# Attention by pairs of heads: head pairs in both halves of the matmul array, spread over query and gate panels

## The chip, the cores and the metric

One core of a Trainium2 chip runs the whole program. Its engines are TensorE (PE, matmuls into the eight PSUM banks; PEld in the profile is its weight load), VectorE (DVE), ScalarE (ACT), GpSimd (POOL) and SyncE (SP, which issues the large DMAs). Each engine works through its own list of instructions in order and waits on semaphores. The metric is the device time of one execution in microseconds; lower is better.

## The reference

Three blocks in fp32 on 256 tokens with 2048 features: a state-space layer, a sliding-window attention with shared keys and values, and a second model with neighbourhood attention and a large MLP. The change touches the sliding-window attention alone: 32 heads of 64 features, four key heads, window 128, so that the first 128 queries see 128 keys and the second 128 queries see 256.

```python
def _swa_sink_attention(q, k, v, sinks):
    ...
    s = jnp.einsum("bcqhrd,bckhd->bchrqk", qb, kk).astype(jnp.float32) * (hd ** -0.5)
    ...
    s = jnp.where(valid[None, :, None, None], s, -jnp.inf)
    sk = sinks.astype(jnp.float32)[None, None, :, :, None, None]
    m = jnp.maximum(jnp.max(s, axis=-1, keepdims=True), sk)
    p = jnp.exp(s - m)
    p = p / (jnp.sum(p, axis=-1, keepdims=True) + jnp.exp(sk - m))
    o = jnp.einsum("bchrqk,bckhd->bcqhrd", p.astype(vv.dtype), vv)
    return o.reshape(bsz, seqlen, hk * rq * hd)

def _swa_mixer(x, k, v, cos, sin, w_in, q_bias, sinks, w_out):
    bsz, seqlen, _ = x.shape
    proj = x @ w_in
    q = (proj[..., :Q_WIDTH] + q_bias).reshape(bsz, seqlen, KV_HEADS, Q_PER_KV, ATT_HEAD_DIM)
    gate = proj[..., Q_WIDTH:]
    q = _rope_partial(q, cos[:, :, None, None, :], sin[:, :, None, None, :])
    o = _swa_sink_attention(q, k, v, sinks.reshape(KV_HEADS, Q_PER_KV))
    o = o * jax.nn.silu(gate)
    return o @ w_out
```

## The kernel before

All large products go by weight **units**: 256 rows by 512 columns of weights, 512 KB. A unit lands in `raw` (a ring of four, `RING`), ScalarE rounds it into `whi` (`split_hi`), VectorE takes the rest into `wlo` (`split_lo`), and TensorE multiplies: high by high, high by low and low by high, so that fp32 precision comes from three passes of the faster format. A panel of 512 columns is eight units (`UPP`). A **token unit** (`token_unit`) has tokens in the rows of the output, 12 matmuls of 512 columns; a **feature unit** (`feature_unit`) has features in the rows, 24 matmuls of 256. The two accumulators, banks 0 and 1 and banks 2 and 3, take turns by panel. ScalarE rounds unit u + 4 when TensorE is done with unit u, which frees the place; VectorE follows.

The stage of the change is, in order: four query panels (32 token units), four gate panels (32 feature units), and the first panel of the output projection (`wo`, 8 token units), whose left operand is the gated attention output in `xh` and `xl`.

Before, the queries of all 32 heads are gathered in `qt`; VectorE adds the bias to each panel and rotates all of them at the end (`rotate`). Then attention runs in **slots**, one for each unit of gate and output panel: slot j is unit j of these 40, and after its matmuls TensorE does a piece of attention. Slot 2 turns all keys and queries to feature rows (`qk_turn`, 40 transposes, copied by ScalarE in `qk_by_feature`). Head h starts in slot h + 3: `scores(h)` puts the mask into a bank (4 or 5) by a product with the identity and adds the scores by products over 64 rows of the array, the upper or lower half by the parity of h. VectorE takes the row maxima (`maximum`), ScalarE the exponentials from the bank with their sums (`weights`), VectorE divides (`scaled_weights`). Two slots later TensorE turns the weights into bank 6 (`weights_turned`, three transposes), VectorE copies them (`weights_by_key`), and a slot later the value products fill half of the rows of bank 7 (`values`), a head to 64 columns of the array. ScalarE keeps a pair's output (`output_kept`), VectorE multiplies it with the activated gate (`gated`), and the pair of `gated_hi` and `gated_lo` splits it for the output projection, from slot 31 on.

The order is written out by hand, as numbers of slots in `HEAD0`, `GATED_AT` and `SPLIT_AT`; the loops over j at the end of each engine's stage walk them. An fp32 product of the scores or values is one instruction in the program's order and two passes on TensorE; a transpose is one.

Of the kernel before, what the change touches and what calls it, by code (L numbers as in the profile page):

```python
# [28 lines left out]
F32R = mybir.dt.float32r  # L29
# [5 lines left out]
P = 128  # L35
# [126 lines left out]
def program(nc, xT, x, pos, conv_w, conv_b, dt_bias, a_log, d_skip, norm_w, w_in, w_out, kv_w, kv_b, b_in,  # L162
# [3 lines left out]
    with es:  # L166
# [23 lines left out]
        identr = place("identr", [P, P], F32R)  # L190
# [11 lines left out]
        mask = place("mask", [P, 3 * P], F32R)  # L202
# [36 lines left out]
        maskf = place("maskf", [P, 3 * P], at=yh_at + 4 * KT * T)  # L239
# [29 lines left out]
        oT = place("oT", [P, KT, T], at=R)  # L269
# [3 lines left out]
        qT = place("qT", [P, AH // 2, T])  # L273
        kT = place("kT", [P, KVH, T])
        Pm = place("Pm", [P, 2, 3 * P])
# [3 lines left out]
        rope = [place(f"rope{n}", [P, TT, AH, HALF]) for n in range(4)]  # L279
# [3 lines left out]
        mx = place("mx", [P, AH, 2])  # L283
        nm = place("nm", [P, AH, 2])
        rs = place("rs", [P, AH, 2])
        esk = place("esk", [P, AH, 2])
        rden = place("rden", [P, AH, 2])
# [205 lines left out]
        def _(pool):  # L493
            g = Steps(S("pool_step"))
            a = g.done(pool.memset(ident[:], 0.0))
            b = g.done(pool.memset(maskf[:], 0.0))
# [17 lines left out]
            for n, op, sign in ((0, ALU.is_ge, -1), (1, ALU.is_gt, 1), (2, ALU.is_ge, -1)):  # L514
                v = maskf[:, n * P:(n + 1) * P]
                pool.affine_select(out=v, in_=v, compare_op=op, fill=NEG, base=0, pattern=[[sign, P]],
                                   channel_multiplier=-sign)
# [90 lines left out]
            norm_rows(1, GATE + 2, 4, "ln1_in")  # L608
# [57 lines left out]
        def _(act):  # L666
# [22 lines left out]
            act.wait_ge(S("ident_ready"), 1)  # L689
            act.activation(identr[:], ident[:], ACT.Copy)  # L690
            act.activation(mask[:], maskf[:], ACT.Copy).then_inc(S("constr_ready"), 1)
# [142 lines left out]
            splits(Q, 4)  # L834

# [8 lines left out]
            def qk_by_feature():  # L844
                for n in range(2 + AH // 4):
                    act.wait_ge(S("qk_mm"), n + 1)
                    dst = tile(kT, 2 * n, 2) if n < 2 else tile(qT, 2 * (n - 2), 2)
                    act.activation(dst, ps[:, 4 + n % 4, :], ACT.Copy).then_inc(S("qk_turned"), 1)

            def weights(h):  # L850


                act.wait_ge(S("nm_ready"), h + 1)
                wait(act, "pt_ready", h - 1)
                b = 4 + h % 2
                act.activation(Pm[:, h % 2, 0:P], ps[:, b, 0:P], ACT.Exp, bias=nm[:, h, 0:1], scale=SWA_SCALE,
                               accum_out=rs[:, h, 0:1])
                act.activation(Pm[:, h % 2, P:3 * P], ps[:, b, P:3 * P], ACT.Exp, bias=nm[:, h, 1:2], scale=SWA_SCALE,
                               accum_out=rs[:, h, 1:2])

                act.activation(esk[:, h, :], nm[:, h, :], ACT.Exp, bias=snk[:, h:h + 1]).then_inc(S("p_ready"), 1)

            def output_kept(n):

                act.wait_ge(S("o_done"), 2 * n + 2)
                act.activation(oT[:, n, :], ps[:, 7, (n % 2) * T:(n % 2 + 1) * T], ACT.Copy).then_inc(S("o_read"), 1)
# [5 lines left out]

            for j in range(ASLOTS):
                h = j - HEAD0
                split_hi(act, GATE + RING + j, 0)
                if j == HEAD0 - 1:
                    qk_by_feature()
                if j == GATE_UNITS - 1:

                    act.wait_ge(S("unit_done"), WO)  # L880
                    gated_hi(0)
                    gated_hi(1)
                if 0 <= h < AH:
                    weights(h)
                if 4 <= h and h % 2 == 0 and h // 2 - 2 < AH // 2:
                    output_kept(h // 2 - 2)
                if j % UPP == 0 and 0 < j <= GATE_UNITS:
                    gate_silu(j // UPP - 1)
                if j >= GATE_UNITS:
                    for n, at in enumerate(SPLIT_AT):  # L890
                        if at == j:
                            gated_hi(n)
# [157 lines left out]
        def _(pe):  # L1050
# [218 lines left out]
            token_panels(Q, L_Q, 4, 0)  # L1269
            def qk_turn():  # L1270

                pe.wait_ge(S("rope_done"), 1)
                for n in range(2 + AH // 4):

                    wait(pe, "qk_turned", n - 3)
                    for e in range(2):
                        for m in range(TT):
                            src = kd[:, m, 2 * n + e].rearrange("p a b -> p (a b)") if n < 2 else \
                                qt[:, m, (2 * (n - 2) + e) * P:(2 * (n - 2) + e + 1) * P]
                            last = pe.transpose(ps[:, 4 + n % 4, e * T + m * P:e * T + (m + 1) * P], src, ident[:])  # L1280
                    last.then_inc(S("qk_mm"), 1)
# [852 lines left out]
```

## Time and profile before

| | |
|---|---|
| median of 3 runs | 2247.25 us (2246.58 to 2249.1) |
| the profiled execution | 2246.58 us, its span 2244.8 us |
| TensorE busy | 2194.2 us, 98% |
| VectorE busy | 1342.5 us, 60% |
| ScalarE busy | 1070.9 us, 48% |
| mean granted TensorE clock | 0.995 |

The span runs from the first to the last instruction. The profile gives busy time of each engine and, in the timeline, the start and the duration of each instruction. Matmuls are pipelined: a duration of 0.39 us may stand beside starts 0.23 us apart, so costs on TensorE are read from start to start. A name such as `ps` is the PSUM tensor with all eight banks.

### The profile page before, as it was taken

The page shows a single profiled execution, that of the slowest core. Times are in us where ns is not written, and L with a number is a line of the kernel's source. Part 1 is how long each engine was busy: PE and PEld are TensorE (multiplying, and loading weights), DVE is VectorE, ACT ScalarE, POOL GpSimd, SP SyncE. Part 2 cuts the span into 40 slices and gives each one's busy share as a digit, 9 for nine tenths or more (in the row PEclk, how much of TensorE's full clock was granted, in tenths as well). Part 3 has the DMA queues.
Part 4 walks back from the last instruction along what each step waited for, and adds up shares of the span by engine and source line. Part 5 has one row for each costly group of instructions (what it writes and reads, how often), then busy time and mean ns, then how long its engine had stood idle before and what let it go on. Part 6 is the DMA issues. An engine that isn't in the chain of part 4 may idle for free.

```text
span 2244.8 us, 36327 instructions
## 1 busy us (share of the span) xinstructions
PE 2194.2 (98%) x13614; PEld 1953.9 (87%) x13614; DVE 1342.5 (60%) x1731; ACT 1070.9 (48%) x1407; POOL 130.7 (6%) x136
## 2 busy tenths in 40 slices
PE   7999999999998999999899999999999999999999
PEld 7999989998887888887788878789989989988987
DVE  5677676776545666665676666655555455554554
ACT  4434357776333435454345455545434444443442
POOL 1000001111000100000005210000000000000000
PEclk9999999999999999999999999999999999999999
DMA  7755655554655764334576644455556556656654
GB/s 229 237 177 177 188 188 179 179 171 160 228 192 173 229 195 132 112 112 152 168 216 195 191 139 138 133 189 171 183 196 186 179 195 187 182 192 189 184 188 159
DMA packets 207026, 402.45 MB, mean 179 GB/s; under 512 B 16132, under 2 KB 18308, under 8 KB 206676
## 3 DMA queue, kind: packets, MB, share of 16 engines
q1 hardware_dynamic: 199168, 385.92, 55.2%
q0 software_dynamic: 4096, 14.50, 2.0%
q8 instruction: 64, 1.05, 0.2%
q10 hardware_dynamic: 3668, 0.73, 0.2%
q14 instruction: 30, 0.25, 0.0%
HBM read 395.27 MB, written 5.83 MB: 179 GB/s over the span
## 4 chain that ended last, share of the span: by engine, by line
PE 90%; DVE 4%; ACT 3%; issue 1%; DMA 1%; POOL 1%; ACTq 0%; SPq 0%; DVEq 0%
PE ps L383 16%; PE ps L385 15%; PE ps L384 15%; PE ps L368 12%; PE ps L370 12%; PE ps L369 12%; ACT whi L350 1%; DMA raw<-w_in 1%; PE ps L1128 1%; DVE wlo L355 1%; PE ps L1315 1%; PE ps L1220 1%; PE ps L1295 1%; PE ps L1294 1%; PE ps L1391 1%
## 5 line engine op out<-in xcount | busy, mean ns | idle before, releaser
L355 DVE TENSOR_TENSOR wlo<-raw,whi 128x1024 fp32r<-128x1024 f32 x712 | 875.4, 1234 | 753.0 <-ACT whi L350 748.6
L350 ACT ACTIVATE whi<-raw 128x1024 fp32r<-128x1024 f32 x712 | 753.0, 1059 | 1071.2 <-PE ps L385 593.6
L368 PE MATMUL ps<-xh,whi 128*128 128x256 f32 x2560 | 734.7, 287 | 17.5 <-DVE wlo L355 16.2
L369 PE MATMUL ps<-xl,whi 128*128 128x256 f32 x2560 | 726.2, 284 | 0.0
L370 PE MATMUL ps<-xh,wlo 128*128 128x256 f32 x2560 | 726.0, 284 | 0.0
L368 PEld LDWEIGHTS ps<-xh,whi 128*128 128x128 f32 x2560 | 492.6, 192 | 28.0 <-issue 20.7
L369 PEld LDWEIGHTS ps<-xl,whi 128*128 128x128 f32 x2560 | 492.9, 193 | 0.2
L370 PEld LDWEIGHTS ps<-xh,wlo 128*128 128x128 f32 x2560 | 492.8, 192 | 0.0
L383 PE MATMUL ps<-whi,xh 128*128 128x512 f32 x792 | 318.7, 402 | 5.8 <-DVE xl L1871 3.1
L384 PE MATMUL ps<-wlo,xh 128*128 128x512 f32 x792 | 310.0, 391 | 0.0
L385 PE MATMUL ps<-whi,xl 128*128 128x512 f32 x792 | 309.9, 391 | 0.0
L383 PE MATMUL ps<-whi,ah 128*128 128x512 f32 x512 | 199.3, 389 | 0.0
L384 PE MATMUL ps<-wlo,ah 128*128 128x512 f32 x512 | 199.3, 389 | 0.0
L385 PE MATMUL ps<-whi,al 128*128 128x512 f32 x512 | 199.3, 389 | 0.0
L383 PEld LDWEIGHTS ps<-whi,xh 128*128 128x128 f32 x792 | 149.6, 189 | 38.5 <-DVE xl L1871 3.7
L385 PEld LDWEIGHTS ps<-whi,xl 128*128 128x128 f32 x792 | 149.6, 189 | 32.3
L384 PEld LDWEIGHTS ps<-wlo,xh 128*128 128x128 f32 x792 | 149.8, 189 | 30.2
L385 PEld LDWEIGHTS ps<-whi,al 128*128 128x128 f32 x512 | 96.2, 188 | 20.0
L384 PEld LDWEIGHTS ps<-wlo,ah 128*128 128x128 f32 x512 | 96.2, 188 | 19.8
L383 PEld LDWEIGHTS ps<-whi,ah 128*128 128x128 f32 x512 | 96.2, 188 | 19.8
L383 PE MATMUL ps<-whi,yh 128*128 128x512 f32 x248 | 96.8, 390 | 0.0
L384 PE MATMUL ps<-wlo,yh 128*128 128x512 f32 x248 | 96.5, 389 | 0.0
(243 smaller groups left out, 1651.1 us busy)
## 6 DMA issues: line engine op xcount, KB each, us to landing
raw<-w SPq DMA_DIRECT2D x256, 512.0 KB, 3.6
raw<-w_in SPq DMA_DIRECT2D x160, 512.0 KB, 4.2
raw<-w_qkv SPq DMA_DIRECT2D x96, 512.0 KB, 4.3
raw<-w_out SPq DMA_DIRECT2D x64, 512.0 KB, 3.7
raw<-b_in SPq DMA_DIRECT2D x64, 512.0 KB, 4.3
raw<-b_out SPq DMA_DIRECT2D x32, 512.0 KB, 3.8
raw<-w_o SPq DMA_DIRECT2D x32, 512.0 KB, 3.6
cumb<-cum_scratch SPq DMA_DIRECT2D x16, 512.0 KB, 4.2
```

Source lines behind the costliest of these rows:

```text
L350: act.activation(whi[:, u % RING], raw[:, u % RING], ACT.Copy).then_inc(S("hi_ready"), 1)
L355: dve.tensor_tensor(wlo[:, u % RING], raw[:, u % RING], whi[:, u % RING].bitcast(F32), ALU.subtract).then_inc(S("lo_ready"), 1)
L368: pe.matmul(o, w_h, ah[:, k, :], start=(k == 0 and n % 2 == 0), stop=False, skip_group_check=True)
L369: pe.matmul(o, w_h, al[:, k, :], start=False, stop=False, skip_group_check=True)
L370: last = pe.matmul(o, w_l, ah[:, k, :], start=False, stop=(k == KT - 1), skip_group_check=True)
L383: pe.matmul(o, x_h, whi[:, u % RING, t, :], start=(k == 0), stop=False)
L384: pe.matmul(o, x_h, wlo[:, u % RING, t, :], start=False, stop=False)
L385: last = pe.matmul(o, x_l, whi[:, u % RING, t, :], start=False, stop=(k == kts - 1))
L1128: last = pe.matmul(ps[r:r + HD, 3, c0 + lo:c0 + hi], xc[:, g % 2, k, f:f + HD], m, start=first, stop=not first, skip_group_check=True)
L1220: last = pe.transpose(ps[:, 4 + kp % 4, n * T + m * P:n * T + (m + 1) * P], src[:, m, k * P:(k + 1) * P], ident[:])
L1294: pe.matmul(ps[:, b, 0:P], q_[:, 0:P], k_[:, 0:P], start=False, stop=True, skip_group_check=True)
L1295: pe.matmul(ps[:, b, P:3 * P], q_[:, P:T], k_, start=False, stop=True, skip_group_check=True).then_inc(S("s_ready"), 1)
```

## The change

Heads go by pairs, and attention begins in the query panels. There are now 72 slots, over query, gate and first output panel. Each query panel is given its bias and rotated as soon as it is done (`query_panel`). Keys are turned in slot 9. Pair p has its scores in slot 12 + 3p, its queries turned three slots before (into bank 6, copied by ScalarE to one of two places of `qT`), its weights turned four and five slots after, its values six slots after. The scores of both heads stand in turn in the list, from the two row halves into banks 4 and 5; those of the values from the two column halves into bank 7. The mask is no longer a product on TensorE: VectorE adds it while it moves the scores of both heads from the banks to `Pm`, where ScalarE takes the exponentials in place. The copy of turned weights (`weights_by_key`) moves from VectorE to ScalarE. The normalising pieces of the rows (`norm_row`) move from query panels 2 and 3 to the slots 32 to 47. The gated outputs 0 to 5 are split in slots 57 to 62 and the last two in slot 66; before, two of them in slot 31, two in 32, two in 33 and one each in 35 and 38, which are output units 0, 1, 3 and 6.

```diff
@@ -77,12 +77,19 @@
-HEAD0 = 3
-ASLOTS = GATE_UNITS + UPP
-
-GATED_AT = [4 * n + HEAD0 + 7 for n in range(AH // 4)]
-SPLIT_AT = [GATE_UNITS - 1, GATE_UNITS - 1, GATE_UNITS, GATE_UNITS, GATE_UNITS + 1, GATE_UNITS + 1, GATE_UNITS + 3,
-            GATE_UNITS + 6]
+AP = AH // 2
+PPK = AP // KVH
+ASLOTS = 2 * GATE_UNITS + UPP
+GATE_AT, WO_AT = GATE_UNITS, 2 * GATE_UNITS
+KEYS_AT, PAIR0, STRIDE = UPP + 1, 12, 3
+SCORES_AT = [PAIR0 + STRIDE * p for p in range(AP)]
...
+TURNED_AT = [(at + 4, at + 5) for at in SCORES_AT]
+VALUES_SLOT = [at + 6 for at in SCORES_AT]
...
@@ -841,29 +837,35 @@
+            def weights(p):
+
+                act.wait_ge(S("nm_ready"), p + 1)
+                for e in range(2):
+                    for c, v in enumerate((Pm[:, p % 2, e, 0:P], Pm[:, p % 2, e, P:3 * P])):
+                        act.activation(v, v, ACT.Exp, bias=nm[:, p, c, e:e + 1], scale=SWA_SCALE,
+                                       accum_out=rs[:, p, c, e:e + 1])
+                act.activation(esk[:, p], skd[:, p], ACT.Exp).then_inc(S("p_ready"), 1)
+
+            def weights_by_key(p, e):
+
+                act.wait_ge(S("pt_ready"), 2 * p + e + 1)
+                wait(act, "o_done", p)
+                act.activation(PTm[:, e], ps[:, 6, 0:3 * P], ACT.Copy).then_inc(S("pts_ready"), 1)
...
-                pe.matmul(ps[:, b, 0:3 * P], identr[:], mask[:], start=True, stop=False,
-                          skip_group_check=True)
-                pe.matmul(ps[:, b, 0:P], q_[:, 0:P], k_[:, 0:P], start=False, stop=True, skip_group_check=True)
-                pe.matmul(ps[:, b, P:3 * P], q_[:, P:T], k_, start=False, stop=True,
-                          skip_group_check=True).then_inc(S("s_ready"), 1)
...
+            def scores(p):
+
+                pe.wait_ge(S("k_turned"), 2)
+                pe.wait_ge(S("q_turned"), p + 1)
+                wait(pe, "s_read", p)
+                for c in range(TT):
+                    for e in range(2):
+                        r = HD * e
+                        q_, k_ = qT[r:r + HD, p % 2, c * P:(c + 1) * P], kT[r:r + HD, p // PPK, 0:(c + 1) * P]
+                        last = pe.matmul(ps[:, 4 + e, c * P:c * P + (c + 1) * P], q_, k_, start=(c == 0), stop=True,
+                                         skip_group_check=True)
+                last.then_inc(S("s_ready"), 1)
...
+            def values(p):
+
+                pe.wait_ge(S("pts_ready"), 2 * p + 2)
+                wait(pe, "o_read", p)
+                k0 = (KVH + p // PPK) * HD
+                c0 = p % 2 * T
+                for m, lo in ((0, 0), (1, P)):
+                    for e in range(2):
+                        r_ = HD * e
+                        w = PTm[:, e, 0:T] if m == 0 else PTm[:, e, T:3 * P]
+                        last = pe.matmul(ps[r_:r_ + HD, 7, c0 + lo:c0 + T], kvt[:, m, k0:k0 + HD], w, start=(m == 0),
+                                         stop=(m == 1), skip_group_check=True)
+                last.then_inc(S("o_done"), 1)
...
+            def maximum(p):
+
+                dve.wait_ge(S("s_ready"), p + 1)
+                wait(dve, "pt_ready", 2 * (p - 1))
+                v = Pm[:, p % 2]
+                s = d.done(dve.tensor_tensor(v, ps[:, 4:6, 0:3 * P], mask[:].unsqueeze(1).to_broadcast([P, 2, 3 * P]),
+                                             ALU.add))
...
             for j in range(ASLOTS):
...
+                split_lo(dve, Q + RING + j, 0)
+                if j < GATE_AT and j % UPP == UPP - 1:
+                    query_panel(j // UPP)
+                for p in range(AP):
+                    if j == SCORES_AT[p]:
+                        maximum(p)
+                    if j == SCORES_AT[p] + 2:
+                        scaled_weights(p)
+                if X1_AT <= j < X1_AT + 2 * UPP:
+                    norm_row(j - X1_AT, "ln0_in", "x1_rows")
```

The lines of the program after the change are numbered one higher for the helpers (L356 for L355 and so on). In the rows below a matmul row stands for one line's product, whose two passes are not told apart.

TensorE, one slot of before in the middle of the gate panels, from the last matmul of the unit on: one head turned, the next but one scored, the one before given its values.

```order
L370 MATMUL ps<-xh,wlo 128x256
L1303 MATMUL ps<-ident,Pm 128x128 [waits pts_ready,p_scaled]
L1303 MATMUL ps<-ident,Pm 128x128 x2
L1292 MATMUL ps<-mask,identr 128x384 [waits p_ready]
L1294 MATMUL ps<-kT,qT 128x128
L1295 MATMUL ps<-kT,qT 128x256
L1315 MATMUL ps<-PTm,kvt 64x256 [waits pts_ready]
L1317 MATMUL ps<-PTm,kvt 64x128
```

TensorE after the change, slot 18, the first with all three: values of pair 0, scores of pair 2, queries of pair 3, then the next unit.

```order
L386 MATMUL ps<-whi,xl 128x512
L1323 MATMUL ps<-PTm,kvt 64x256 [waits pts_ready]
L1323 MATMUL ps<-PTm,kvt 64x256
L1323 MATMUL ps<-PTm,kvt 64x128 x2
L1300 MATMUL ps<-kT,qT 128x128 [waits s_read,q_turned,k_turned]
L1300 MATMUL ps<-kT,qT 128x128
L1300 MATMUL ps<-kT,qT 128x256 x2
L1288 MATMUL ps<-ident,qt 128x128 [waits pts_ready,rope_done]
L1288 MATMUL ps<-ident,qt 128x128
L384 MATMUL ps<-whi,xh 128x512 [waits lo_ready,x_ready]
```

The mask product is gone, the products of two heads stand side by side, and the turn of the weights has gone to the two slots between.

ScalarE before, two slots in the gate panels (names: `Pm` weights, `rs` their sums, `esk` the sink's term, `oT` the output kept).

```order
L856 ACTIVATE Pm,rs<-ps,nm 128x128 [waits nm_ready]
L858 ACTIVATE Pm,rs<-ps,nm 128x256
L861 ACTIVATE esk<-nm,snk 128x2
L866 ACTIVATE oT<-ps 128x256 [waits o_done]
L350 ACTIVATE whi<-raw 128x1024 [waits unit_done,landed2]
L856 ACTIVATE Pm,rs<-ps,nm 128x128 [waits pt_ready,nm_ready]
```

ScalarE after, slots 16 to 18: the exponentials of pair 1 stand between the two copies of turned weights of pair 0.

```order
L351 ACTIVATE whi<-raw 128x1024 [waits unit_done,landed0]
L863 ACTIVATE PTm<-ps 128x384 [waits pt_ready]
L855 ACTIVATE Pm,rs<-Pm,nm 128x128 [waits nm_ready]
L855 ACTIVATE Pm,rs<-Pm,nm 128x256
L855 ACTIVATE Pm,rs<-Pm,nm 128x128
L855 ACTIVATE Pm,rs<-Pm,nm 128x256
L857 ACTIVATE esk<-skd 128x4
L351 ACTIVATE whi<-raw 128x1024 [waits unit_done,landed1]
L863 ACTIVATE PTm<-ps 128x384 [waits pt_ready]
L351 ACTIVATE whi<-raw 128x1024 [waits unit_done,landed2]
L868 ACTIVATE oT<-ps 128x256 [waits o_done]
L848 ACTIVATE qT<-ps 128x256 [waits q_mm]
```

The copies were VectorE's before, and each head's exponentials had a slot of their own; now one slot in three has four of them.

VectorE before, one slot of the gate panels.

```order
L1835 TENSOR_REDUCE mx<-ps 128x1 [waits s_ready]
L1836 TENSOR_REDUCE mx<-ps 128x1
L1838 SCALAR_TENSOR_TENSOR nm<-mx,nsnk 128x2 [waits dve_step]
L1846 COPY PTm<-ps 128x384 [waits o_done,pt_ready]
L355 TENSOR_TENSOR wlo<-raw,whi 128x1024 [waits hi_ready]
```

VectorE after, slot 15: the second query panel stands before the maxima of pair 1.

```order
L1836 TENSOR_TENSOR qt<-ps,qbias 128x512 [waits qb_in1,unit_done]
L1836 TENSOR_TENSOR qt<-ps,qbias 128x512
...
L1799 TENSOR_TENSOR qt<-rope_131,rope_132 128x2x8x8 [waits dve_step]
L1800 TENSOR_TENSOR qt<-rope_133,rope_134 128x2x8x8
L1848 TENSOR_TENSOR Pm<-ps,mask 128x768 [waits dve_step,s_ready]
L1852 TENSOR_REDUCE mx<-Pm 128x2 [waits dve_step]
L1853 TENSOR_REDUCE mx<-Pm 128x2
L1856 SCALAR_TENSOR_TENSOR nm<-mx,nsnk 128x4 [waits dve_step]
L1858 TENSOR_TENSOR skd<-nm,nsnk 128x4 [waits dve_step]
```

The copy is gone and the add with the mask has come; a panel's bias and rotation now lie between a pair's scores and its maxima.

## Rows read from the trace of the kernel before

**Rows 1.** Busy time (and instructions) of each engine, gate panels with attention.

```profile
core 0: us, PE busy (x) PEld busy (x) DVE busy (x) ACT busy (x) POOL busy (x), PEclk, DMA share, GB/s
860.00:1003.00 143.00, 142.98 (x989) 119.86 (x987) 91.42 (x254) 75.48 (x195) 3.75 (x7) 1.00 0.39 117
```

**Rows 2.** Timeline, TensorE: start us, duration, instruction [idle before]; ends of stages, waits.

```profile
752.74 0.39 PE L383 MATMUL ps<-whi,xh 128*128 128x512 f32 x1
...
839.78 0.28 PE L368 MATMUL ps<-xh,whi 128*128 128x256 f32 x1
...
854.66 0.39 PE L368 MATMUL ps<-xh,whi 128*128 128x256 f32 x1 [1.30 <-ACT qT L848]
...
1036.76 0.80 PE L383 MATMUL ps<-whi,xh 128*128 128x512 f32 x1 [3.07 <-DVE xl L1871]
...
1041.14 0.39 PE L383 MATMUL ps<-whi,xh 128*128 128x512 f32 x1
```

**Rows 3.** Timeline, TensorE: one head's slot in the gate panels.

```profile
906.65 0.28 PE L370 MATMUL ps<-xh,wlo 128*128 128x256 f32 x1
906.77 0.49 PE L1303 MATMUL ps<-ident,Pm 128*128 128x128 f32 x3
907.01 0.42 PE L1292 MATMUL ps<-mask,identr 128*128 128x384 f32 x1
907.37 0.48 PE L1294 MATMUL ps<-kT,qT 64*128 64x128 f32 x2
...
908.22 0.65 PE L1315 MATMUL ps<-PTm,kvt 128*64 128x256 f32 x2
...
909.01 0.39 PE L368 MATMUL ps<-xh,whi 128*128 128x256 f32 x1
...
911.98 0.49 PE L1303 MATMUL ps<-ident,Pm 128*128 128x128 f32 x3
```

**Rows 4.** Timeline, TensorE: a pair of heads in the state-space stage.

```profile
504.60 0.28 PE L370 MATMUL ps<-xh,wlo 128*128 128x256 f32 x1
504.80 0.87 PE L1128 MATMUL ps<-Mm,xc 128*64 128x256 f32 x8
505.61 0.39 PE L368 MATMUL ps<-xh,whi 128*128 128x256 f32 x1
```

**Rows 5.** Timeline, TensorE: four transposes in each token slot, key and value panel.

```profile
731.72 0.60 PE L1220 MATMUL ps<-ident,xtok 128*128 128x128 f32 x4
...
734.93 0.60 PE L1220 MATMUL ps<-ident,xtok 128*128 128x128 f32 x4
```

**Rows 6.** Timeline, ScalarE: split, exponentials of a head, output kept.

```profile
907.03 1.06 ACT L350 ACTIVATE whi<-raw 128x1024 fp32r<-128x1024 f32 x1 [1.98 <-PE ps L370]
909.18 0.37 ACT L856 ACTIVATE Pm<-ps,nm 128x128 f32<-128x128 f32 x1 [1.09 <-DVE nm L1838]
...
910.17 0.38 ACT L866 ACTIVATE oT<-ps 128x256 f32<-128x256 f32 x1
```

**Rows 7.** Timeline, VectorE: maxima, copy, split, scaling, gating in one slot.

```profile
908.32 0.29 DVE L1835 TENSOR_REDUCE mx<-ps 128x1 f32<-128x128 f32 x1 [1.94 <-PE ps L1295]
...
909.06 0.56 DVE L1846 COPY PTm<-ps 128x384 f32<-128x384 f32 x1
909.53 1.22 DVE L355 TENSOR_TENSOR wlo<-raw,whi 128x1024 fp32r<-128x1024 f32 x1
910.66 0.15 DVE L1851 TENSOR_TENSOR rs<-rs,esk 128x2 f32<-128x2 f32 x1
...
911.52 0.68 DVE L1865 TENSOR_TENSOR oT<-oT,gT 128x512 f32<-128x512 f32 x1
```

**Rows 8.** Timeline, VectorE: bias and rotation of the key and value panel.

```profile
755.23 1.28 DVE L1770 TENSOR_TENSOR kvt<-ps,kvbias 128x512 f32<-128x512 f32 x2
...
757.72 0.43 DVE L1794 COPY kd<-kvt 128x512 f32<-128x512 f32 x1
```

**Rows 9.** Groups of instructions: busy us, mean ns, idle before; ScalarE's exponential tables.

```profile
L856 ACT ACT_TABLE_LOAD x5 | 6.4, 1283 | 0.1
```

More of the change, by code:

```diff
@@ L201, in program @@
         xl = place("xl", [P, KT, T], F32R)
-        mask = place("mask", [P, 3 * P], F32R)
+        mask = place("mask", [P, 3 * P])
         mask01 = place("mask01", [P, 3 * P])
@@ L278, in program @@
         kvbias = place("kvbias", [P, PANEL])
-        rope = [place(f"rope{n}", [P, TT, AH, HALF]) for n in range(4)]
+        rope = [place(f"rope{n}", [P, TT, PANEL // HD, HALF]) for n in range(4)]
         lnrow = place("lnrow", [P, 2, D])
@@ L1268, in _, with keys_turned @@
             entry_panel(KV, L_KV, 0, 0)
[L1269 to L1275, printed above, removed]
+            def keys_turned():
+                pe.wait_ge(S("k_ready"), 1)
+                for n in range(2):
                     for e in range(2):
                         for m in range(TT):
[L1278 to L1281, printed above, removed]
-                pe.wait_ge(S("qk_turned"), 2 + AH // 4)
@@ L1298, in weights_turned, with queries_turned @@
-            def weights_turned(h):
-                pe.wait_ge(S("p_scaled"), h + 1)
-                wait(pe, "pts_ready", h)
+                            last = pe.transpose(ps[:, 4 + n, e * T + m * P:e * T + (m + 1) * P],
+                                                kd[:, m, 2 * n + e].rearrange("p a b -> p (a b)"), ident[:])
+                    last.then_inc(S("k_mm"), 1)
+            def queries_turned(p):
+                pe.wait_ge(S("rope_done"), p // PPK + 1)
+                wait(pe, "pts_ready", 2 * sum(b < QUERIES_AT[p] for _, b in TURNED_AT))
+                for m in range(TT):
+                    last = pe.transpose(ps[:, 6, m * P:(m + 1) * P], qt[:, m, p * P:(p + 1) * P], ident[:])
+                last.then_inc(S("q_mm"), 1)
@@ new lines, in _ @@
+                if j == KEYS_AT:
+                    keys_turned()
+                for p in range(AP):
+                    if j == VALUES_SLOT[p]:
+                        values(p)
+                    for e in range(2):
+                        if j == TURNED_AT[p][e]:
+                            weights_turned(p, e)
+                for p in range(AP):
+                    if j == SCORES_AT[p]:
+                        scores(p)
+                    if j == QUERIES_AT[p]:
+                        queries_turned(p)
@@ L1793, in _ @@
                     .to_broadcast([P, KVH, 2, HD])
-                dve.tensor_copy(kd[:, m], src)
+                last = dve.tensor_copy(kd[:, m], src)
+            last.then_inc(S("k_ready"), 1)
+            dve.wait_ge(S("mask_ready"), 3)
+            s = d.done(dve.tensor_scalar(nsnk[:], snk[:], -1.0, None, ALU.mult))
+            d.wait(dve, s)
             def norm_row(i, sem, out):
@@ L1854, in scaled_weights @@
                 d.wait(dve, s)
-                for m, v in enumerate((Pm[:, h % 2, 0:P], Pm[:, h % 2, P:3 * P])):
-                    last = dve.tensor_scalar(v, v, rden[:, h, m:m + 1], None, ALU.mult)
+                sink = nsnk[:, 2 * p:2 * p + 2].unsqueeze(1).to_broadcast([P, TT, 2])
+                s = d.done(dve.scalar_tensor_tensor(nm[:, p], mx[:, p], -SWA_SCALE, sink, ALU.mult, ALU.min))
+                d.wait(dve, s)
+                dve.tensor_tensor(skd[:, p], nm[:, p], sink, ALU.subtract).then_inc(S("nm_ready"), 1)
@@ new lines, in scaled_weights @@
+            def scaled_weights(p):
+                dve.wait_ge(S("p_ready"), p + 1)
+                s = d.done(dve.tensor_tensor(rs[:, p], rs[:, p], esk[:, p], ALU.add))
+                d.wait(dve, s)
+                s = d.done(dve.reciprocal(rden[:, p], rs[:, p]))
+                d.wait(dve, s)
+                for c, v in enumerate((Pm[:, p % 2, :, 0:P], Pm[:, p % 2, :, P:3 * P])):
+                    r = rden[:, p, c, :].unsqueeze(2).to_broadcast([P, 2, (c + 1) * P])
+                    last = dve.tensor_tensor(v, v, r, ALU.mult)
```

194 lines of the change are left out of this document (67 added, 127 removed).

## The prediction

> **What bounds the kernel now.** I read the page first: TensorE is busy for 98% of the span, so time can only be won where it does work that isn't needed, does it singly, or stands. The stretch view [rows 1] says the same of the attention stage: TensorE 142.98 of 143.00 us busy at a granted clock of 1.00, VectorE 91 and ScalarE 75. So in this stage neither of the two helpers is the limit; TensorE's own list of instructions is. I then took starts of single matmuls from the timeline, since a start-to-start distance is what an instruction really costs (durations overlap).
>
> The stage from the first query unit to the second output panel runs from 752.74 to 1041.14, 288.40 us [rows 2]. It holds 72 weight units. A token unit costs 2.72 us: 32 of them fill 752.74 to 839.78 [rows 2]. A feature unit is 24 matmuls at a step of 0.12 us [rows 3], 2.88 us. So the units alone need 32 x 2.72 + 32 x 2.88 + 8 x 2.72 = 200.96 us, and **attention costs 87.4 us of TensorE's time on top**. Where those sit:
> - Each head's slot: from the last matmul of the unit, 906.65, to the first of the next, 909.01, is 2.36 us instead of 0.12, and the first matmul after it gives the next 0.10 us late, 2.34 us in all. Inside [rows 3]: three transposes 0.24, the mask product 0.36, scores 0.85 (907.37 to 908.22), values 0.79. Both of the last two end in a drain, since the array is reshaped after them. 25 slots follow this pattern exactly; slots at both ends hold parts of it.
> - The turn of all queries and keys, 40 transposes in one block, with a wait of 1.30 us for ScalarE's copies behind it [rows 2]: this slot is 6.35 us longer than its unit.
> - The last gated outputs: TensorE stands 3.07 us for VectorE's split, and comes back slow (a matmul of 0.80 instead of 0.39 us) [rows 2]; the slot has 4.9 us over its unit, a last value product among them.
>
> **The change, part by part, on TensorE.**
> 1. *Values of a pair in the two column halves.* The trace has this very form: the state-space stage issues eight passes, two heads in alternation, of the same shapes. They take 0.80 us from the first to the next unit [rows 4], drain included, against 0.79 for one head here. So the pair costs what one head does. I take 0.80, and 0.08 for entering (504.60 to 504.80, less a step of 0.12).
> 2. *Scores of a pair in the two row halves.* No row shows row halves in alternation. Bounds: 0.85 a pair if they run side by side as the column halves do, 1.70 if one after the other. I take 0.85, since nearest to it in kind is [rows 4], where even the two passes of each fp32 product found their partner; the two heads also write different banks.
> 3. *The mask product* (32 x 0.36 = 11.5 us) leaves TensorE. VectorE gets an add of 768 elements a pair.
> 4. *Transposes.* Four of them lengthen a token slot to 3.21 us (731.72 to 734.93) [rows 5], 0.49 over 2.72, so 0.123 each, bare. Their number stays, 96 + 32 + 8.
> 5. *Fewer changes of the array's shape*: one round trip a pair, not one a head. After a drain the first weight load isn't covered, 0.10 us.
>
> So a slot with values, scores and two query transposes costs 0.08 + 0.80 + 0.85 + 0.25 + 0.10 = 2.08 us; there are 14. Two slots have no values yet (1.28 each), two have values only (0.98 each). Together 29.1 + 2.6 + 2.0 = 33.7. The 96 weight transposes, three in a slot, cost 11.8; eight for the keys and two for the first queries 1.2. **Sum 46.7 us, if TensorE never waits.** The gated outputs are now split at slots 57 to 62 and 66; output unit c = 6 needs the last of them at slot 70, and ScalarE's and VectorE's part of slot 66 is some 3.5 us, so the 3.07 us wait goes and nothing is late in its place. The wait behind the block of turns goes too: a pair's queries are copied three slots before use.
>
> **New waits.** They come from the in-order queue of ScalarE, which takes the copies of turned weights from VectorE. The tight spot is the slot after the scores. From the end of its unit ScalarE does: the split 1.0 (1.06 with its latency), a copy of 384 elements 0.4, four exponentials with their sums and the sink 1.8 (one head 0.99 [rows 6], twice, less one sink), the next split 1.0, the second copy 0.5: 4.7 us. TensorE wants that copy for the values after two units and two groups of transposes: 2 x (2.72 + 0.37) = 6.2 us, 6.5 in the gate panels. Cover is 1.5 to 1.8 us, and steady pairs wait nothing. VectorE does a pair in 7.6 of about 11 us: three splits 3.4 to 3.7; add and maxima 2.4 (0.74 a head [rows 7], and 0.9 for the add, by 0.68 for 512 elements); scaling 1.5 to 1.7 (0.86 a head). With the normalising pieces (0.7 a slot in slots 32 to 47, as 512 elements in [rows 7]) it is 9.7 of 11.4. Nothing on it is due within its lag. Two places break the cover:
> - Pair 0 and 1. The first exponential reads its table, 1.28 us [rows 9], and slot 15 puts a query panel (2.5 us by the like panel of keys and values [rows 8], 2.8 here as its rotation is twice as long) before the maxima of pair 1. Counted from the end of unit 15 on VectorE: split 1.2, scaling of pair 0 1.5, split 1.2, panel 2.8, add and maxima 2.4; then on ScalarE 1.8, 1.0 and 0.5: 12.4. (VectorE still has the split before, since ScalarE's table load held it up.) TensorE is there at 1.3 + 3 x 2.72 + 2 x 0.37 = 10.2. **Wait 2.2 us.**
> - The three gate activations at slots 40, 48 and 56 (a table load of 1.28 and two activations of some 0.6, an estimate between 0.38 for 256 and 1.06 for 1024 elements [rows 6], and 1.28 again for the next exponential). Less the cover: 0.9, 1.1 and 0.3. **Wait 2.3 us.**
>
> I take 4.5 us of waits. Bounds: none (if each queue is 1 us quicker at these places), and 11, if the cover is also short by 0.4 us in each of 16 pairs. Pool and SyncE get no new instruction; SyncE's transfers of weights, 117 GB/s here [rows 1], come sooner by a fifth and still have four slots each.
>
> **The sum** against the profiled execution's own 2246.58 us (span 2244.8): 87.4 - 46.7 - 4.5 = 36.2 us less, **2210.4 us**. The median of the three runs is 0.67 us above that execution, so I say 2210.5.
>
> The Trainium skill, "TensorE: Matmul & The Clock Gate", Part 3, reports 3.07x for four row tiles rather than 4x. Estimated from that share (0.77), a pair of scores would take 1.10 us, not 0.85, and the time would be some 4 us more, 2214; no row here has row tiles side by side. The same part says that weight loads overlap running matmuls only when the row group differs. [Rows 4] don't agree: there both heads use all 128 rows and differ in columns alone, and the eight passes still take one head's time.
>
> **Rivals.**
> - *R1, row halves don't run side by side, or only in part.* Each fp32 product is two passes, and both heads' weights come as 128 columns. For it: no row shows it. Against it: [rows 4]. Cost up to 0.85 x 16 = 13.6 us, of which about 2 come back since the waits shrink: 2215 to 2222.
> - *R2, the helpers' cover is short.* The add reads two banks at once and the exponentials work in place; were these 20% dearer than the rows, each pair waits some 0.4 to 1 us: 2216 to 2228.
> - *R3, slower than before.* One mechanism: the value product stands for the second copy in every pair, because ScalarE has the exponentials between the two copies. To use up 36 us it must stand 2.3 us a pair, so ScalarE's chain must be 8.5 instead of 4.7 us: decided if a table were loaded at each change between copy and exponential (2 x 1.28 a pair, and more). Against it: 32 heads now show five loads in all [rows 9], with copies between the exponentials. Had it, with stalls that bring the clock down as after the 3.07 us wait, the time would be 2250 to 2260.
> - *R4, the change doesn't do what it says*: pairs gain nothing in either half. [Rows 4] exclude it for values; what is left is R1 at its end.
>
> **How the numbers follow.** Forecast as summed, waits 0 to 7 us: 0.62, 2206 to 2213. R1: 0.20. R2: 0.13. R3: 0.02, and 0.03 for a gain that is eaten elsewhere. Range to hold 8 in 10: below by the sum with no wait and a row pair a little cheaper than a single, 2205; above into R1's end and R2's middle, 2222. A difference under 0.2% (4.5 us) can't be told from none. Faster 0.96, same 0.02, slower 0.02.
>
> **What would show it.** On TensorE: the stage from first query unit to second output panel at 252 us, not 288; slots in a rhythm of three, 2.08, 0.37 and 0.37 us above their unit; eight score passes in 0.85 us (R1: 1.2 to 1.7); no wait behind key turns, none at the output panel. Waits named as value products for ScalarE's copy, once near pair 0 and near slots 40 and 48, and not in each pair (R2, R3). Table loads for exponentials: four. I would be wrong if the stages outside these 72 units changed by more than 1 us: the change has nothing there but two small ScalarE copies less at the start.

## The result and the profile after

| | before | changed |
|---|---|---|
| median of four runs | 2247.73 us (2246.58 to 2249.1) | 2209.82 us (2207.97 to 2209.99) |
| profiled execution, its span | 2246.58, 2244.8 us | 2209.81, 2208.1 us |
| TensorE busy | 2194.2 us, 98% | 2158.4 us, 98% |
| first query unit to second output panel | 288.40 us | 250.75 us |

The ratio is 0.983, with a 95% interval of 0.981 to 0.985: 38 us less, and 36.8 us between the two profiled executions. The stage lost 37.65 us. Elsewhere 0.95 us came on top: the first query unit starts at 753.44 instead of 752.74, and 0.25 us more lies behind the stage.

The timeline of TensorE after the change (start us, duration, instruction, idle before it), the ends of the stage; it answers to [rows 2]:

```profile
753.44 0.39 PE L384 MATMUL ps<-whi,xh 128*128 128x512 f32 x1
...
1004.19 0.39 PE L384 MATMUL ps<-whi,xh 128*128 128x512 f32 x1
```

One slot with values, scores and queries in the gate panels, and one with transposes of weights; they answer to [rows 3]:

```profile
919.29 0.28 PE L371 MATMUL ps<-xh,wlo 128*128 128x256 f32 x1
919.41 0.49 PE L1310 MATMUL ps<-ident,Pm 128*128 128x128 f32 x3
919.66 0.36 PE L369 MATMUL ps<-xh,whi 128*128 128x256 f32 x1
...
925.69 0.28 PE L371 MATMUL ps<-xh,wlo 128*128 128x256 f32 x1
925.89 0.87 PE L1323 MATMUL ps<-PTm,kvt 128*64 128x256 f32 x8
926.70 0.93 PE L1300 MATMUL ps<-kT,qT 64*128 64x128 f32 x8
927.55 0.44 PE L1288 MATMUL ps<-ident,qt 128*128 128x128 f32 x2
927.75 0.36 PE L369 MATMUL ps<-xh,whi 128*128 128x256 f32 x1
```

The values of a pair take 0.81 us (925.89 to 926.70), the scores of a pair 0.85 (to 927.55), each for two heads what one head took before (0.79 and 0.85). From unit to unit the slot has 2.01 us over its unit in the gate panels, 2.06 to 2.09 in the query panels; a slot with three transposes has 0.31 to 0.32 in the gate panels and 0.35 to 0.40 in the query panels.

All waits of TensorE in the stage that the timeline shows, the values at their place:

```profile
812.01 1.25 PE L1323 MATMUL ps<-PTm,kvt 128*64 128x256 f32 x8 [2.26 <-ACT PTm L863]
813.19 1.66 PE L1300 MATMUL ps<-kT,qT 64*128 64x128 f32 x8
814.77 0.69 PE L1288 MATMUL ps<-ident,qt 128*128 128x128 f32 x2
...
903.32 0.87 PE L1323 MATMUL ps<-PTm,kvt 128*64 128x256 f32 x8 [0.77 <-ACT PTm L863]
...
971.23 0.87 PE L1323 MATMUL ps<-PTm,kvt 128*64 128x256 f32 x8 [0.30 <-ACT PTm L863]
```

The first is pair 0, at slot 18, and it costs more than it shows: behind it the eight score passes take 1.58 us to the next row instead of 0.85, since the clock has fallen. The view by stretches (columns as in [rows 1]) has a mean granted clock of 0.66 for these 5 us, part of them at 1.2 GHz and part at 2.4, against 1.00 from 785 to 812 and from 817 on; the first row is a stretch without long waits, for comparison:

```profile
860.00:982.00 122.00, 120.93 (x1019) 112.61 (x1019) 92.75 (x158) 80.00 (x181) 4.29 (x8) 1.00 0.53 157
812.00:817.00 5.00, 4.99 (x25) 3.45 (x26) 4.78 (x9) 1.67 (x3) 0.00 (x0) 0.66 0.69 192
```

The slot has 5.66 us over its unit, where its neighbours have 2.06 to 2.09, and the slot behind it 0.67 where the like ones have 0.39. That is 3.85 us more in all: 2.26 of wait and 1.6 of slow passes.

Why pair 0 waits is seen on VectorE and ScalarE. VectorE gets to pair 1's maxima late, behind pair 0's scaling, a split and the whole query panel; ScalarE stands for it:

```profile
801.05 1.03 DVE L1869 TENSOR_TENSOR Pm<-Pm,rden 128x256 f32<-128x256 f32 x2
802.00 1.22 DVE L356 TENSOR_TENSOR wlo<-raw,whi 128x1024 fp32r<-128x1024 f32 x1
803.13 1.28 DVE L1836 TENSOR_TENSOR qt<-ps,qbias 128x512 f32<-128x512 f32 x2
...
806.14 0.96 DVE L1848 TENSOR_TENSOR Pm<-ps,mask 128x768 f32<-128x768 f32 x1 [0.15 <-DVE qt L1800]
```

```profile
808.68 0.40 ACT L855 ACTIVATE Pm<-Pm,nm 128x128 f32<-128x128 f32 x1 [3.61 <-DVE skd L1858]
...
810.54 1.04 ACT L351 ACTIVATE whi<-raw 128x1024 fp32r<-128x1024 f32 x1
811.49 0.47 ACT L863 ACTIVATE PTm<-ps 128x384 f32<-128x384 f32 x1
```

The groups of instructions (busy us, mean ns) give the new operations: the add with the mask at 0.95 us, put at 0.9, and the copy of turned weights at 0.47, put at 0.4 to 0.5. There are four table loads for exponentials where [rows 9] had five:

```profile
L1848 DVE TENSOR_TENSOR Pm<-ps,mask 128x768 f32<-128x768 f32 x16 | 15.2, 951 | 0.2 <-DVE qt L1800 0.2
L863 ACT ACTIVATE PTm<-ps 128x384 f32<-128x384 f32 x32 | 15.1, 472 | 0.0
L855 ACT ACT_TABLE_LOAD x4 | 5.1, 1283 | 0.1
```

### The profile page after: what moved, and what is told of

Read it like the earlier page. It is cut to its first block, busy times and chain, and to the rows that moved or that the text cites. A ratio compares the mean times of both kernels' runs of the same rounds, so it can differ in the third digit from the quotient of the medians.

```text
span 2208.1 us, 36192 instructions
## 1 busy us (share of the span) xinstructions
PE 2158.4 (98%) x13582; PEld 1931.9 (87%) x13582; DVE 1336.4 (61%) x1637; ACT 1078.1 (49%) x1429; POOL 130.9 (6%) x136
## 4 chain that ended last, share of the span: by engine, by line
PE 89%; DVE 4%; ACT 3%; issue 2%; DMA 1%; POOL 1%; ACTq 0%; SPq 0%; DVEq 0%
PE ps L384 15%; PE ps L386 15%; PE ps L385 15%; PE ps L369 12%; PE ps L370 12%; PE ps L371 12%; ACT whi L351 1%; DMA raw<-w_in 1%; DVE wlo L356 1%; PE ps L1131 1%; PE ps L1223 1%; PE ps L1300 1%; PE ps L1323 1%; PE ps L1404 1%; PE ps L1380 1%
## 5 line engine op out<-in xcount | busy, mean ns | idle before, releaser
L356 DVE TENSOR_TENSOR wlo<-raw,whi 128x1024 fp32r<-128x1024 f32 x712 | 875.6, 1234 | 777.2 <-ACT whi L351 772.3
L386 PE MATMUL ps<-whi,yl 128*128 128x512 f32 x248 | 96.6, 389 | 0.0
```

Of the source, the lines that this page charges most:

```text
L356: dve.tensor_tensor(wlo[:, u % RING], raw[:, u % RING], whi[:, u % RING].bitcast(F32), ALU.subtract).then_inc(S("lo_ready"), 1)
L386: last = pe.matmul(o, x_l, whi[:, u % RING, t, :], start=False, stop=(k == kts - 1))
```

## The experiments

The time agreed with the forecast, so the question was whether its terms did. The first theory was that of the sum: both halves of the array work side by side, the rest is fewer changes of shape, and the waits come from the order on VectorE and ScalarE. Its rivals were that the pairs are cheap for another reason, and that the waits have another source. All stages below are read as above, from the first query unit to the second output panel; the changed kernel has 250.75 us there, and 250.83 when it was run again.

| kernel | stage, us | time, us |
|---|---|---|
| scores of a pair in one row half | 259.39 | 2217.82 |
| values of a pair in one column half | 261.55 | 2221.80 |
| both in one half | 269.41 | 2229.72 |
| scores listed head by head | 250.88 | 2212.02 |
| before, without the mask product | 281.57 | 2241.29 |
| values a slot later | 249.37 | 2209.36 |
| outputs split late | 261.75 | 2219.35 |
| changed kernel again (median of 5) | 250.83 | 2208.72 |
| query panel behind the maxima (median of 5) | 246.99 | 2205.46 |
| and gate activations moved (median of 5) | 245.75 | 2204.43 |

Times without a note are of one run. They scatter more than the stages, because the start of the first query unit moves by itself, from 752.06 to 755.55 us in the kernels made from the changed one, with nothing changed ahead of it. Part of that is TensorE's clock far ahead of the stage: where the mean granted clock from 95 to 110 us is 0.77 the unit starts at 753.8 to 755.6, where it is 0.89 or 1.00 at 752.1 to 753.4. So the stage decides. It was read from one trace of each kernel.

### Scores from one row half

```diff
                 for c in range(TT):
                     for e in range(2):
-                        r = HD * e
+                        r = 0
                         q_, k_ = qT[r:r + HD, p % 2, c * P:(c + 1) * P], kT[r:r + HD, p // PPK, 0:(c + 1) * P]
```

> From the changed kernel; both heads of a pair take their score operands from the lower 64 rows (head 1 is given head 0's), so the two row halves are never in use together; all else stays. Theory (row halves run side by side): each pair's eight score passes take 1.70 us instead of 0.85, the stage of 72 units gets 16 x 0.85 = 13.6 us longer less some 1 to 2 us of waits that shrink: stage 250.8 to about 263, time about 2221 to 2223. Rival (the pair is cheap for another reason, such as fewer changes of shape): the eight passes stay near 0.85 and the time within 2 us of 2209.8.

TensorE's timeline of this kernel:

```profile
860.51 1.57 PE L1300 MATMUL ps<-kT,qT 64*128 64x128 f32 x8
862.01 0.44 PE L1288 MATMUL ps<-ident,qt 128*128 128x128 f32 x2
```

1.50 us instead of 0.85. The row halves do run side by side. But the loss is 0.65 a pair and 8.6 us for the stage, not 0.85 and 12 to 13. The eight passes in a row have one drain at their end as the four had, and I had doubled it with the passes: 16 pairs at 0.65 are 10.4 us. Of these some 2 came back at pair 0:

```profile
813.04 0.87 PE L1323 MATMUL ps<-PTm,kvt 128*64 128x256 f32 x8 [1.60 <-ACT PTm L863]
```

TensorE comes later and waits 1.60 us instead of 2.26, and behind this wait the granted clock stays at 1.00, so the 1.6 us of slow passes are gone as well.

### Values through one column half

```diff
-                        r_ = HD * e
+                        r_ = 0
                         w = PTm[:, e, 0:T] if m == 0 else PTm[:, e, T:3 * P]
```

> From the changed kernel; both heads of a pair write their values through the lower 64 columns to the same 64 rows of bank 7, so the upper column half stays unused and head 0's output is overwritten. Theory (column halves run side by side): the eight value passes take 0.79 x 2 less one drain of 0.2, 1.4 us, instead of 0.80: stage longer by some 9.5 to 12 us, time 2218 to 2222. Rival (side by side makes no difference, the shape's drain is the cost): under 2 us.

```profile
861.76 1.51 PE L1323 MATMUL ps<-PTm,kvt 128*64 128x256 f32 x8
863.20 0.93 PE L1300 MATMUL ps<-kT,qT 64*128 64x128 f32 x8
```

1.44 us instead of 0.81, the stage 10.8 us longer: as the theory had it. Pair 0's wait is again 2.26 us here, with the clock down behind it, so nothing comes back.

### Both in one half

Both edits above together.

> From the changed kernel; the scores of both heads come from the lower row half and the values of both go through the lower column half, so nothing runs side by side (head 1's results are not those of its rows, head 0's output is overwritten). What is left of the change is then the mask's move, one change of shape a pair for one a head, the spread over query panels and the early split. Theory (the parts add): 250.8 + 8.6 + 10.8 = 270.2 us for the stage, with up to 2 us less or more of waits, time about 2229; against the kernel before without its mask product (281.6 us) the 11 us that remain are 16 round trips of the shape saved at some 0.6 us and the two waits. Rival (the two halves do not add, since one hides the other): stage under 266.

```profile
863.78 1.51 PE L1323 MATMUL ps<-PTm,kvt 128*64 128x256 f32 x8
865.23 1.57 PE L1300 MATMUL ps<-kT,qT 64*128 64x128 f32 x8
```

269.41 us: 18.7 more than the changed kernel, where the two alone gave 8.6 and 10.8. The parts add to within 0.8 us. What is left of the change without any side-by-side work still beats the kernel before without its mask product, 281.57 us, by 12 us. The slots say where from: there two heads cost 2 x 2.15 = 4.30 us; here a pair, its queries' transposes included, costs 3.31 + 0.31 + 0.32 = 3.94. Without the two transposes (0.25) that is 0.6 us a pair, some 10 us in 16 pairs, and the order of the work says for what: two heads apart change the array's shape six times, a pair three times, so three changes at 0.2 us. The rest is waits. Gone are 1.30 us behind the block of turns, 0.53 at the start of the output panel and 3.07 at its end; come are 1.61, 0.77 and 0.31 ahead of value products; 2.2 us less. So the 37.65 us that the stage lost divide into three steps: 6.8 from the kernel before to the one without its mask product (below), 12.2 from there to this kernel, and 18.7 from here to the changed one, for work side by side.

### Scores listed head by head

```diff
-                for c in range(TT):
-                    for e in range(2):
+                for e in range(2):
+                    for c in range(TT):
                         r = HD * e
```

> From the changed kernel; the scores of a pair are listed head by head (first both products of head 0, then both of head 1) and not in alternation. Each half is still used by one head. Theory A (TensorE starts passes strictly in the order of the list): the second head can only overlap the last pass of the first, the eight passes take about 1.3 to 1.5 us and the time grows by 7 to 10 us. Theory B (it takes passes for the free half from further down the list): 0.85 us and no change, within 1 us.

```profile
860.45 0.93 PE L1300 MATMUL ps<-kT,qT 64*128 64x128 f32 x8
861.32 0.44 PE L1288 MATMUL ps<-ident,qt 128*128 128x128 f32 x2
```

0.87 us, the stage 0.1 us longer. Theory A is out: no alternation in the list is needed. The starts of the single passes say the same: they come in twos, 0.01 us apart, and the four passes of 128 columns of both heads start before any of 256, though the list has both long passes of head 0 ahead of head 1's short ones. Whether TensorE itself or something on the way to it makes this order, the starts don't tell. The time is 2.2 us above the changed kernel's, and all of it lies ahead of the stage (its first query unit is 2.1 us later), which this edit doesn't touch.

### The kernel before, without the mask product

```diff
-                pe.matmul(ps[:, b, 0:3 * P], identr[:], mask[:], start=True, stop=False,
-                          skip_group_check=True)
-                pe.matmul(ps[:, b, 0:P], q_[:, 0:P], k_[:, 0:P], start=False, stop=True, skip_group_check=True)
+                pe.matmul(ps[:, b, 0:P], q_[:, 0:P], k_[:, 0:P], start=True, stop=True, skip_group_check=True)
```

> From the kernel before; the product of identity and mask is left out (scores are not masked), nothing else. Theory: its cost is its place in TensorE's list, 0.36 us a head, so 32 x 0.36 = 11.5 us less: 2235.1 us. If the weight load of the scores product behind it had been hidden in the mask product or the drain differs, 8 to 10 us. Rival (the slot is bound by VectorE or ScalarE): under 2 us.

```profile
906.29 0.49 PE L1301 MATMUL ps<-ident,Pm 128*128 128x128 f32 x3
906.71 0.49 PE L1292 MATMUL ps<-kT,qT 64*128 64x128 f32 x2
```

The stage is 6.8 us shorter, not 11.5. In [rows 3] the distance from the mask product to the scores is 0.36 us, but 0.2 of it is the drain ahead of the change to 64 rows. Without the product the drain comes behind the transposes: from the first of them to the scores it is 0.42 us now and was 0.60 (906.77 to 907.37). So the mask cost 0.18 to 0.19 us a head, just under 6 us. The rest is at the end of the output panel, and it is not the wait, which is as long as before, 3.07 us; it is the clock behind it:

```profile
1032.78 0.50 PE L383 MATMUL ps<-whi,xh 128*128 128x512 f32 x1 [3.07 <-DVE xl L1869]
```

```profile
1032.50:1037.50 5.00, 4.72 (x21) 3.91 (x22) 0.73 (x2) 1.06 (x1) 0.85 (x1) 1.00 0.31 105
```

The granted clock stays at 1.00 here; in the kernel before, it is 0.66 from 1036.50 to 1041.50, behind the same wait. That is 1.5 us, and 0.5 is lost again in waits at two other slots. Of the 6.8 us just under 6 are the mask's.

### Values a slot later

```diff
-VALUES_SLOT = [at + 6 for at in SCORES_AT]
+VALUES_SLOT = [at + 7 for at in SCORES_AT]
```

> From the changed kernel; the values of a pair come seven slots after its scores, not six, so values and scores stand in different slots and TensorE changes its shape and back 32 times, not 18. Theory: each extra round trip costs a drain (0.2) and an uncovered weight load (0.1), less what the joint slot already pays: 14 x 0.18 to 0.3 = 2.5 to 4 us more, less up to 3 us since the copy has a slot more and the waits of 3.3 us (and 1.6 us of slow matmuls behind the first) go: between 2 us less and 2 us more than 2209.8. The slots show it: the score slot 1.28 us over its unit, the value slot 0.37 + 0.98.

Score slots have 1.21 to 1.28 us over their unit, value slots 1.26 to 1.32 with three transposes. The three slots of a pair come to 2.99 us in the query panels, against 2.80 to 2.86 in the changed kernel, and to 0.15 more in the gate panels too. So a second visit costs 0.15 us a pair, some 2 us in all, and less than I had for it. I had counted a whole round trip more. But the joint slot changes shape three times (into column halves, to row halves, back) and two slots apart change it four times: one change more. The waits of 0.77 and 0.30 us are gone, and that of pair 0 is now 1.50 us and stands ahead of the queries' transposes, for the same copy:

```profile
814.01 0.41 PE L1288 MATMUL ps<-ident,qt 128*128 128x128 f32 x2 [1.50 <-ACT PTm L863]
```

Its slow passes are gone, the granted clock is 1.00 behind it. Together the stage is 1.4 us shorter, and the time is level with the changed kernel's, inside the bounds given.

### Outputs split late

```diff
-SPLIT_AT = [max(GATED_AT[n] + 1, WO_AT - UPP + n + 1) for n in range(UPP)]
+SPLIT_AT = [WO_AT - 1, WO_AT - 1, WO_AT, WO_AT, WO_AT + 1, WO_AT + 1, WO_AT + 3, WO_AT + 6]
```

> From the changed kernel; the gated outputs are split at the slots of before (two in 63, 64 and 65, then 67 and 70). Theory: the output panel's last unit waits again for the split of slot 70 on ScalarE and VectorE, 3.1 us, and its first matmuls are slow: 3.9 us more in the last slot, stage 254.7, time 2213.5. Rival (before, the wait was due to attention work in the same slots, which is gone): under 0.5 us.

```profile
983.01 0.47 PE L384 MATMUL ps<-whi,xh 128*128 128x512 f32 x1 [2.32 <-issue]
...
990.85 0.50 PE L384 MATMUL ps<-whi,xh 128*128 128x512 f32 x1 [2.13 <-DVE xl L1884]
...
1009.46 0.79 PE L384 MATMUL ps<-whi,xh 128*128 128x512 f32 x1 [3.07 <-DVE xl L1884]
```

11.0 us, nearly three times what the theory gave. The last wait came as it said, 3.07 us and 1.9 of slow passes. But the late split now stalls TensorE three times. In the kernel before, attention still ran beside the first output units (2.4 us of TensorE's work in each slot), and TensorE waited no more than 0.35 us for the splits of slots 31 to 33, where it now waits 2.32 and 2.13. As the edit changes only when the splits are made, the account is that moving attention forward takes their cover away. So the early split is not a refinement that saves 4 us: in the new order it is what keeps 11 us of the gain.

### The query panel behind the maxima, and the gate activations moved

In the loop of VectorE, and in the second kernel also of ScalarE:

```diff
-                if j < GATE_AT and j % UPP == UPP - 1:
-                    query_panel(j // UPP)
                 for p in range(AP):
                     if j == SCORES_AT[p]:
                         maximum(p)
                     if j == SCORES_AT[p] + 2:
                         scaled_weights(p)
+                if j < GATE_AT and j % UPP == UPP - 1:
+                    query_panel(j // UPP)
```

```diff
+SILU_AT = [GATE_AT + 9, GATE_AT + 18, GATE_AT + 27, WO_AT]
-GATED_AT = [max(VALUES_SLOT[2 * n + 1], GATE_AT + UPP * (n // 2 + 1)) + 1 for n in range(UPP)]
+GATED_AT = [max(VALUES_SLOT[2 * n + 1], SILU_AT[n // 2]) + 1 for n in range(UPP)]
...
-                if j > GATE_AT and j <= WO_AT and j % UPP == 0:
-                    gate_silu((j - GATE_AT) // UPP - 1)
+                if j in SILU_AT:
+                    gate_silu(SILU_AT.index(j))
```

The changed kernel, as reference beside them:

> The changed kernel as it is, as reference for the three beside it: 2209.8 us, within 1 us.

> From the changed kernel; on VectorE the bias and rotation of a query panel come behind the maxima and the scaling of the same slot. Theory: the 2.26 us wait of pair 0's values comes from the 3 us of the panel ahead of pair 1's maxima, and the slow matmuls behind it (1.6 us) from the wait: both go, stage 250.8 to 246.9, time 3.9 us less, 2206.0. Rival (the wait comes from the first table load or ScalarE's queue): the wait stays over 1 us and the gain is under 2 us.

> As panel_behind, and the gate activations move from slots 40, 48, 56 to 41, 50, 59, behind the second copy of turned weights; the gating of outputs follows by the same slots. Theory: the waits of 0.77 and 0.30 us go too, 1.1 us less than panel_behind, 2204.9, some 5 us under the changed kernel. Rival (the table load then makes the next copy late instead): no change against panel_behind, or up to 1 us more.

Medians of five: 2208.72 (2207.79 to 2209.01; 1.1 us under the figure expected), 2205.46 (2204.35 to 2206.22) and 2204.43 us (2203.56 to 2206.26). Against the kernel before these are 0.983, 0.9816 (0.9802 to 0.9829) and 0.9814 (0.980 to 0.9827). The same slot 18 in the kernel with the panel behind, without wait and at full clock:

```profile
810.37 0.87 PE L1323 MATMUL ps<-PTm,kvt 128*64 128x256 f32 x8
811.17 0.93 PE L1300 MATMUL ps<-kT,qT 64*128 64x128 f32 x8
812.03 0.44 PE L1288 MATMUL ps<-ident,qt 128*128 128x128 f32 x2
```

Its stage is 3.84 us shorter where 3.9 was expected, 2.26 of wait and 1.6 of slow passes. The rival, ScalarE's first table load, would have kept over 1 us. The second edit takes the waits of 0.77 and 0.30 us away, and 1.24 us off the stage (0.84 and 0.38 in the two slots). By times this last step is within the scatter; by the stage it is there. This version beats both kernels, the changed one by about 4 us.

## Why the prediction was right, and where its terms were off

Forecast 2210.5 us, measured 2209.8; the stage was put at 252 us and is 250.75. The mechanism was right. That the number is off by less than 1 us is in part luck: work was put 1.8 us too high and waits 1.2, the slow passes behind a wait, 1.6, were left out, and 0.95 came on top outside the stage.

- **The base and the units.** 87.4 us of attention in the stage was the right thing to count. After the change it is 49.8.
- **Work, 46.7 us forecast.** 49.8 less 3.3 of waits and 1.6 of slow passes leaves 44.9. The slots with all three parts were put at 2.08 and have 2.06 to 2.09 in the query panels and 2.01 in the gate panels. The term that was too large is that of the transposes: 0.37 us for three, taken from a token slot [rows 5], is right for token units, but beside feature units they cost 0.32. One slot was also counted too full: slot 57 has no query transposes, and 1.82 us where 2.08 was put.
- **Values in both column halves at 0.80.** Measured 0.81, and 1.44 without the halves. The pair in the state-space stage [rows 4] was the right row.
- **Scores in both row halves at 0.85, without a row.** Measured 0.85. R1 is out. Its price was too high, 13.6 us for passes that cost 10.4, since it doubled a drain that is paid once. The 2 us that it had coming back did so at pair 0, mostly because the clock did not fall there.
- **The mask product, "32 x 0.36 = 11.5 us".** Too high by a factor of two: 0.18 to 0.19 a head, 6 us. It did no harm to the total, because the total was the new slots added up, and not the old ones less their parts. Had I subtracted part by part, I would have counted the drain twice and been 5 us too low.
- **The waits, 4.5 us forecast.** Pair 0: 2.2 forecast, 2.26 measured. Slot 40's activation: 0.9 forecast, 0.77. Slot 56's: 0.3, and 0.30, by some luck, since the split of a gated output (0.61 us on ScalarE at 969.24) stands ahead of the same copy and wasn't counted; the edit that took the wait away moved both, so their shares stay open. Slot 48's: 1.1 forecast, none there. At slot 48 ScalarE ends the activation before the next unit does, and the reload of 1.28 alone fits into the cover. Missing from the sum was what a wait costs behind itself: 1.6 us of passes at the lower clock after pair 0's. I had the row for it, the 0.80 us matmul behind the 3.07 us wait [rows 2], and used it for the old wait and not for the new one. Slot 48's missing wait and these passes nearly cancel. Nor is the term fixed: behind 3.07 us in the kernel before the clock fell, and behind the same 3.07 us without the mask product it did not.
- **The cover of steady pairs.** ScalarE's chain from the end of the unit after the scores to the second copy was put at 4.7 us. One round of it, from the start of the split to that of the copy, is 4.2 us with the copy's 0.47 behind:

```profile
884.99 1.06 ACT L351 ACTIVATE whi<-raw 128x1024 fp32r<-128x1024 f32 x1 [2.54 <-PE ps L371]
...
888.18 1.06 ACT L351 ACTIVATE whi<-raw 128x1024 fp32r<-128x1024 f32 x1
889.14 0.47 ACT L863 ACTIVATE PTm<-ps 128x384 f32<-128x384 f32 x1
```

  4.62 us. No steady pair waits, so R2 and R3 are out; exponentials in place cost 393 and 496 ns where they cost 367 and 465 from the bank.
- **The gated outputs.** That the 3.07 us wait goes and nothing comes in its place was right. What the part is worth in the new order, 11 us, the prediction didn't see.
- **Small slips.** The old last slots have 5.1 us over their units, not 4.9, and the median's 0.67 us was named and not added (it would give 2211.1). The sum doesn't rest on either.
- **Nothing outside the stage over 1 us.** 0.95 us, on the edge. No more than the scatter: the same start moves by 3.5 us between kernels that don't differ ahead of it.

The prediction's estimate of 1.10 us for a pair of scores, from the 3.07x that the Trainium skill ("TensorE: Matmul & The Clock Gate", Part 3) gives for four row tiles, is not borne out for the two row tiles here: measured is 0.85, with no loss. The Trainium skill, in the same part, has matmuls start strictly in the order of the list. The scores listed head by head take 0.87 us, and their starts stand in another order than the list, so this case's trace does not agree.

## What to carry to other kernels

When TensorE is the limit, cost a reordered stage by adding up the new slots from rows of like slots, and not by subtracting parts of the old ones: a drain belongs to the change of shape, and whoever takes out one part finds it again behind the next. So count the changes of shape, at 0.15 to 0.2 us each here. Put work that contracts over 64 rows or writes 64 rows in pairs for the two halves; here that made the second head free. Before moving work forward, ask what it covered where it was. And give a wait of over 2 us on TensorE a second term, from nothing to nearly 2 us here, for the slow passes that can stand behind it.

## What the runs showed of the hardware that I had not expected

- Passes for the free half of the array start ahead of others that the list has before them: eight score passes take 0.85 us in alternation and 0.87 head by head.
- A change of the array's shape costs 0.15 to 0.2 us, whichever run one takes it from: 0.6 us for three saved a pair, 0.15 for one added when values and scores were set apart.
- The same wait does not always bring the clock down. Behind 2.26 us (five traces) it fell each time (granted 0.66 over 5 us in the changed kernel), at some 1.6 us. Behind 1.50, 1.60 and 1.61 us it didn't. Behind 3.07 us it fell in the kernel before and with the late split, and not without the mask product; with the late split it fell behind 2.13 us and not behind 2.32. What decides in between stays open.
- Three transposes cost 0.37 us beside token units and 0.32 beside feature units. Why was not tried.
